# A mixture-of-experts layer on one core: an expert's first table holds 96 places instead of 128

## What is computed

```python
scores = sigmoid(xf @ w_router)                      # 512 tokens x 64 experts
choice = scores + router_bias
# best 4 of 8 groups of experts, then the best TOP_K = 8 experts of those
_, idx = top_k(where(emask, choice, -inf), TOP_K)
wts = sel / sum(sel) * 2.5
routed[tok] = sum over its 8 experts e of  w * ((silu(x @ w_gate_e[e]) * (x @ w_up_e[e])) @ w_down_e[e])
x = layer_norm(ALPHA * x + shared + routed, ln2_g, ln2_b)
```

## Time and profile before

| | us |
|---|---|
| median of 3 runs | 1356.36 (1355.73 to 1359.55) |
| the profiled execution, its own time | 1356.58 |
| its span in the profile | 1355.0 |
| TensorE busy in the span | 1281.0 (95%) |
| VectorE busy | 890.0 (66%) |
| ScalarE busy | 712.3 (53%) |
| GpSimd (POOL) busy | 388.0 (29%) |
| granted TensorE clock, mean | 0.978 of full |

### The profile page before, as it was taken

One profiled execution on the slowest core, in us unless ns is written; L12 is line 12 of the kernel. 1 busy time (PEld: TensorE's weight loads), 2 busy tenths in 40 slices (PEclk: granted clock), 3 DMA queues, 4 the chain that ended last, 5 costly groups with the idle time before them and its releaser, 6 DMA issues.

```text
span 1355.0 us, 15040 instructions
## 1 busy us (share of the span) xinstructions
PE 1281.0 (95%) x5608; PEld 933.7 (69%) x5608; DVE 890.0 (66%) x1167; ACT 712.3 (53%) x870; POOL 388.0 (29%) x262
## 2 busy tenths in 40 slices
PE   7999999999899999987999999999999999999965
PEld 4888766666566775553677787777777777777732
DVE  4011255465756564652688888888888888888858
ACT  4333433333233220011588888888887888887710
POOL 3433322122323351144132332223232222323201
PEclk9999999999999999988999999999999999999978
DMA  4922111111111525040799999999999999999776
GB/s 157 321 82 78 59 59 59 40 58 41 59 40 59 201 78 210 17 156 20 258 378 366 378 366 375 372 373 366 373 373 361 369 367 373 374 366 365 272 317 257
DMA packets 68120, 311.30 MB, mean 230 GB/s; under 512 B 17788, under 2 KB 17916, under 8 KB 41552
## 3 DMA queue, kind: packets, MB, share of 16 engines
q1 hardware_dynamic: 48560, 276.64, 54.8%
q0 software_dynamic: 19488, 33.70, 6.6%
HBM read 305.74 MB, written 42.01 MB: 257 GB/s over the span
## 4 chain that ended last, share of the span: by engine, by line
PE 61%; DMA 25%; DVE 5%; ACT 5%; issue 3%; another core or an unknown queue 0%; POOL 0%; SPq 0%; POOLq 0%; DVEq 0%; ACTq 0%
DMA raw<-in_w_gu 23%; PE PS L655 22%; PE PS L897 8%; PE PS L760 4%; PE PS L847 4%; ACT w_hi_e L1126 4%; PE PS L698 4%; PE PS L850 3%; PE PS L844 3%; PE PS L778 3%; PE PS L731 3%; PE PS L709 2%; PE PS L829 1%; DMA parts<-y_d 1%; PE PS L878 1%
## 5 line engine op out<-in xcount | busy, mean ns | idle before, releaser
L1442 DVE TENSOR_TENSOR w_lo_e<-raw,w_hi_e 128x2048 fp32r<-128x2048 f32 x192 | 433.6, 2282 | 4.9 <-ACT w_hi_e L1126 4.8
L1126 ACT ACTIVATE w_hi_e<-raw 128x2048 fp32r<-128x2048 f32 x192 | 368.4, 1920 | 112.3 <-DMA raw<-in_w_gu 72.0
L1670 POOL DMA_INDIRECT y_d<-y_slots,tab x64 | 113.9, 1779 | 425.7 <-PE PS L916 324.4
L1622 POOL TENSOR_TENSOR w_lo<-ring,w_hi 128x1024 fp32r<-128x1024 f32 x54 | 128.4, 2379 | 292.2 <-ACT w_hi L1028 292.2
L847 PE MATMUL PS<-w_hi_e,xs_lo 128*128 128x512 f32 x512 | 144.7, 404 | 0.0
L844 PE MATMUL PS<-w_hi_e,xs_hi 128*128 128x512 f32 x512 | 143.8, 402 | 0.0
L850 PE MATMUL PS<-w_lo_e,xs_hi 128*128 128x512 f32 x512 | 138.7, 392 | 0.0
L1286 DVE CUSTOM_DVE_ANT_0 region<-PS,region 128x128 f32<-128x128 f32 (+1 forms) x64 | 30.6, 478 | 148.7 <-PE PS L698 146.7
L1071 ACT ACTIVATE region<-region,nmax 128x128 f32<-128x128 f32 (+3 forms) x80 | 43.7, 546 | 149.7 <-DVE nmax L1286 149.5
L655 PE MATMUL PS<-x_hi,w_hi 128*128 128x512 f32 x424 | 115.5, 415 | 0.0
L847 PEld LDWEIGHTS PS<-w_hi_e,xs_lo 128*128 128x128 f32 x512 | 91.7, 188 | 33.5 <-DVE xs_lo L1468 16.2
(11 more groups left out here) (177 smaller groups left out, 1853.1 us busy)
## 6 DMA issues: line engine op xcount, KB each, us to landing
raw<-in_w_gu SPq DMA_DIRECT2D x128, 1024.0 KB, 11.2
raw<-in_w_down_e SPq DMA_DIRECT2D x64, 1024.0 KB, 10.8
ring<-in_w_merge SPq DMA_DIRECT2D x32, 640.0 KB, 3.9
ring<-in_w_proj SPq DMA_DIRECT2D x22, 512.0 KB, 3.7
parts<-y_d SPq DMA_DIRECT2D x8, 1024.0 KB, 15.8
parts<-y_d SPq DMA_DIRECT2D x4, 1536.0 KB, 12.7
region<-in_w_out SPq DMA_DIRECT2D x1, 4096.0 KB, 15.1
bias_d<-bias_rows SPq DMA_DIRECT2D x3, 1280.0 KB, 12.1
```

The costliest lines, as they stand in the source:

```text
L1126: nc.scalar.activation(w_hi_e[b][:, lo:hi], raw[b][:, lo:hi], ACT.Copy).then_inc(made, 1)
L1442: nc.vector.tensor_tensor(w_lo_e[b][:, lo:hi], raw[b][:, lo:hi], w_hi_e[b][:, lo:hi].bitcast(F32), ALU.subtract).then_inc(made, 1)
L1622: nc.gpsimd.tensor_tensor(wl, w, wh.bitcast(F32), ALU.subtract).then_inc(w_lo_made, 1)
L1670: pool.indirect_dma_start(y_d, bass.IndirectOffsetOnAxis(ap=rows, axis=0), y_slots[:, b, :], None, bounds_check=last_row, oob_is_err=False ...
```

## The change

The table of an expert holds `CAP` = 96 places. The tables of 96 places that can be needed for 512 tokens are `N_TAB` = 6 in place of 4; `tab_d` is filled with 576 times 64 pairs in place of 512 times 64. All that has one row of an expert per partition (gather, scatter, `x_slots`, `silu`, `h_rows`, `y_slots`, the outputs of gate_up and down) has 96 partitions; all that has the rows as columns (turned rows and their two parts, turned `h` and its two parts, so the stationary operands of gate_up and down) is 96 columns wide. Number and order of instructions stay in the loop over the experts, as do the weights, their split, and the shared expert. The general loop is entered from a list of 97, in place of 129.

```diff
+CAP = 96
+N_TAB = -(-SEQ // CAP)
+TAB_ROWS = -(-N_TAB * CAP // (P // 2)) * (P // 2)
...
+        def rows_of(s):
+            return P if s < QT else CAP
...
-        tab_d = nc.dram_tensor("tab_d", (SEQ * N_EXP, 2), I32).ap()
+        tab_d = nc.dram_tensor("tab_d", (TAB_ROWS * N_EXP, 2), I32).ap()
...
-                to = PS[:, G_BANK + s % 2, :]
+                to = PS[0:CAP, G_BANK + s % 2, :]
                 for c in cs:
-                    nc.tensor.matmul(to, xs_hi[:, b, c, :], wh[:, c, :], start=(c == 0), stop=False)
+                    nc.tensor.matmul(to, xs_hi[:, b, c, 0:CAP], wh[:, c, :], start=(c == 0), stop=False)
...
-                    mm = nc.tensor.transpose(PS[:, H_BANK, half * P:(half + 1) * P], h_of(s % 2)[:, half, :], ident[:, :])
+                    mm = nc.tensor.transpose(PS[:, H_BANK, half * P:half * P + r], h_of(s % 2)[0:r, half, :],
+                                             ident[0:r, 0:r])
...
-                            mm = nc.tensor.matmul(PS[:, Y_BANK + n, :], hx[:, s % 2, half, :],
+                            mm = nc.tensor.matmul(PS[0:CAP, Y_BANK + n, :], hx[:, s % 2, half, 0:CAP],
                                                   w[:, half, n * 512:(n + 1) * 512],
...
-                xs = x_slots[:, e % 2, :].rearrange("p (q c) -> p c q", c=KT)
+                xs = x_slots[0:CAP, e % 2, :].rearrange("p (q c) -> p c q", c=KT)
                 for c in range(KT):
-                    mm = nc.tensor.transpose(PS[:, X_BANK + c // 4, (c % 4) * P:(c % 4 + 1) * P], xs[:, c, :],
-                                             ident[:, :])
+                    mm = nc.tensor.transpose(PS[:, X_BANK + c // 4, (c % 4) * P:(c % 4) * P + CAP], xs[:, c, :],
+                                             ident[0:CAP, 0:CAP])
...
-                nc.scalar.activation(xs_hi[:, e % 2, :, :],
-                                     PS[:, X_BANK:X_BANK + 2, :].rearrange("p a (c n) -> p (a c) n", n=P), ACT.Copy)\
+                nc.scalar.activation(xs_hi[:, e % 2, :, 0:CAP],
+                                     PS[:, X_BANK:X_BANK + 2, :].rearrange("p a (c n) -> p (a c) n", n=P)[:, :, 0:CAP],
+                                     ACT.Copy)\
...
-            with pe.If(n > P):
+            with pe.If(n > CAP):
...
-            tab_rows = tab_d.rearrange("(c p e) b -> c p e b", p=P, e=N_EXP)
+            tab_rows = tab_d[0:N_TAB * CAP * N_EXP, :].rearrange("(c p e) b -> c p e b", p=CAP, e=N_EXP)
             pool.wait_ge(tab_written, 16 * QT * TOP_K)
-            pool.dma_start(tab[:, :, :], tab_rows[0]).then_inc(tab_in, 16)
+            pool.dma_start(tab[0:CAP, :, :], tab_rows[0]).then_inc(tab_in, 16)
...
-                pool.indirect_dma_start(x_slots[:, b, :], None, x1_d, bass.IndirectOffsetOnAxis(ap=rows, axis=0),
+                pool.indirect_dma_start(x_slots[0:CAP, b, :], None, x1_d, bass.IndirectOffsetOnAxis(ap=rows, axis=0),
                                         bounds_check=last_tok, oob_is_err=False).then_inc(done, 16)
...
-                pool.indirect_dma_start(y_d, bass.IndirectOffsetOnAxis(ap=rows, axis=0), y_slots[:, b, :], None,
+                pool.indirect_dma_start(y_d, bass.IndirectOffsetOnAxis(ap=rows, axis=0), y_slots[0:CAP, b, :], None,
                                         bounds_check=last_row, oob_is_err=False).then_inc(done, 16)
...
-                    scatter(tab[:, e, 1:2], e % 2, rows_out[e % 2])
+                    scatter(tab[0:CAP, e, 1:2], e % 2, rows_out[e % 2])
...
-                    gather(tab[:, j, 0:1], j % 2, slots_in[j % 2])
+                    gather(tab[0:CAP, j, 0:1], j % 2, slots_in[j % 2])
```

More of the change, by code:

```diff
@@ L579, in _ @@
             n = sp.value_load(most_i[0:1, 0:1], min_val=0, max_val=SEQ)
-            with sp.If(n > P):
+            with sp.If(n > CAP):
                 sp.wait_ge(y_done, STEPS_MOE)
-                with sp.Fori(1, SEQ // P) as c:
+                with sp.Fori(1, N_TAB) as c:
                     with sp.Fori(0, N_EXP) as e:
@@ L590, in _ @@
                             .then_inc(ov["w"], 16)
-                sp.wait_ge(ov["out"], 16 * (SEQ // P - 1) * N_EXP)
+                sp.wait_ge(ov["out"], 16 * (N_TAB - 1) * N_EXP)
             for b in range(2):
@@ L965, in _ @@
             n = pe.value_load(most_i[0:1, 0:1], min_val=0, max_val=SEQ)
-            with pe.If(n > P):
+            with pe.If(n > CAP):
                 pe.wait_ge(y_out, N_EXP)
                 pe.sem_inc(ov["y"], 1)
-                with pe.Fori(1, SEQ // P) as c:
+                with pe.Fori(1, N_TAB) as c:
                     with pe.Fori(0, N_EXP) as e:
@@ L980, in _ @@
                         for k in range(KT):
-                            mm = nc.tensor.matmul(PS[:, G_BANK, :], xT[:, k, 0:P], gate_up_of(raw[0])[:, k, :],
+                            mm = nc.tensor.matmul(PS[0:CAP, G_BANK, :], xT[:, k, 0:CAP], gate_up_of(raw[0])[:, k, :],
                                                   start=(k == 0), stop=(k == KT - 1))
@@ L985, in _ @@
                         for half in range(FT):
[L986 to L987 removed]
+                            mm = nc.tensor.transpose(PS[:, H_BANK, half * P:half * P + CAP], h_of(0)[0:CAP, half, :],
+                                                     ident[0:CAP, 0:CAP])
                         mm.then_inc(ov["hturn"], 1)
@@ L1189, in _ @@
             n = act.value_load(most_i[0:1, 0:1], min_val=0, max_val=SEQ)
-            with act.If(n > P):
-                with act.Fori(1, SEQ // P) as c:
+            with act.If(n > CAP):
+                with act.Fori(1, N_TAB) as c:
                     with act.Fori(0, N_EXP) as e:
@@ L1462, in low_hT @@
                 dve.wait_ge(hT_made, s + 1)
-                nc.vector.tensor_tensor(hT_lo[:, s % 2, :, :], PS[:, H_BANK, 0:F].rearrange("p (f n) -> p f n", f=FT),
-                                        hT_hi[:, s % 2, :, :].bitcast(F32), ALU.subtract).then_inc(hT_lo_made, 1)
+                nc.vector.tensor_tensor(hT_lo[:, s % 2, :, 0:CAP],
+                                        PS[:, H_BANK, 0:F].rearrange("p (f n) -> p f n", f=FT)[:, :, 0:CAP],
+                                        hT_hi[:, s % 2, :, 0:CAP].bitcast(F32), ALU.subtract).then_inc(hT_lo_made, 1)
             def low_x(e):
                 dve.wait_ge(xs_hi_made, e + 1)
-                nc.vector.tensor_tensor(xs_lo[:, e % 2, :, :],
-                                        PS[:, X_BANK:X_BANK + 2, :].rearrange("p a (c n) -> p (a c) n", n=P),
-                                        xs_hi[:, e % 2, :, :].bitcast(F32), ALU.subtract).then_inc(xs_lo_made, 1)
+                nc.vector.tensor_tensor(xs_lo[:, e % 2, :, 0:CAP],
+                                        PS[:, X_BANK:X_BANK + 2, :].rearrange("p a (c n) -> p (a c) n", n=P)[:, :, 0:CAP],
+                                        xs_hi[:, e % 2, :, 0:CAP].bitcast(F32), ALU.subtract).then_inc(xs_lo_made, 1)
             def base(t):
@@ L1518, in _ @@
             n = dve.value_load(most_i[0:1, 0:1], min_val=0, max_val=SEQ)
-            with dve.If(n > P):
-                with dve.Fori(1, SEQ // P) as c:
+            with dve.If(n > CAP):
+                with dve.Fori(1, N_TAB) as c:
                     dve.wait_ge(ov["tab"], c * 16)
@@ L1676, in _ @@
             for j in range(2):
-                gather(tab[:, j, 0:1], j, slots_in[j])
+                gather(tab[0:CAP, j, 0:1], j, slots_in[j])
             for s in range(3, STEPS_MOE + 2):
@@ L1689, in _ @@
             n = pool.value_load(most_i[0:1, 0:1], min_val=0, max_val=SEQ)
-            with pool.If(n > P):
+            with pool.If(n > CAP):
                 pool.sem_inc(ov["free"], 1)
-                with pool.Fori(1, SEQ // P) as c:
-                    pool.dma_start(tab[:, :, :], tab_rows[bass.ds(c, 1)].rearrange("c p e b -> (c p) e b"))\
+                with pool.Fori(1, N_TAB) as c:
+                    pool.dma_start(tab[0:CAP, :, :], tab_rows[bass.ds(c, 1)].rearrange("c p e b -> (c p) e b"))\
                         .then_inc(ov["tab"], 16)
@@ L1697, in _ @@
                         pool.wait_ge(ov["rows"], j + 1)
-                        gather(rows_u[:, 0:1], 0, ov["in"])
+                        gather(rows_u[0:CAP, 0:1], 0, ov["in"])
                         pool.wait_ge(ov["yout"], j + 1)
-                        scatter(rows_u[:, 1:2], 0, ov["out"])
+                        scatter(rows_u[0:CAP, 1:2], 0, ov["out"])
                         pool.wait_ge(ov["out"], j * 16 + 16)
```

54 lines of the change are left out of this document (30 added, 24 removed).

## The result

| | us | ratio to before, 95% |
|---|---|---|
| before, median of 4 | 1356.53 (1355.73 to 1359.55) | |
| changed, median of 4 | 1386.59 (1381.06 to 1391.05) | 1.0215 (1.0171 to 1.026) |
| changed, profiled execution | 1384.11, span 1382.5 | |

The account below looks back on a forecast made before the run. The busiest DMA engine, with 8 real rows of each 128, was taken to set the 9.89 us period. 1356.58 - 28.5 (loop) - 0.3 (end) = 1327.8 us profiled, so 1327.5 us predicted, range 1317 to 1357.

Parts of the forecast that it names:

- What bound the kernel before: Expert loop: the DMA engine with 8 real rows of each 128 sets the 9.89 us period; TensorE waits 0.53 us.
- Rows per engine: Gathers and scatters: 96 rows put 6 on each engine; the busiest moves 245,760 bytes, 9.27 us at 26.5 GB/s.
- rival B: Slower: 96 rows go to 8 engines, 12 each, 1431 us; includes blocks of 6 hindering each other; chance 0.06.
- What is late next: Expert loop: TensorE at 9.35 us becomes the bound; period 9.44 us with irregular ones, saving 28.5 us.
- Transposes: TensorE, 10 per expert at 0.112 us: no gain taken, up to 0.28 us per expert if streamed columns count.
- Elementwise: ScalarE and VectorE copies: xs_hi falls by 0.22 us, xs_lo by 0.26, hT copies by 0.05 and 0.07; nothing counted.
- Matmuls: TensorE, 36 per expert: still stream 512 columns, 0.91 us for four; no gain.
- POOL and table: Gathers and scatters may give 0 to 0.7 us of POOL; table fill is 288 KB for 256; nothing counted.
- The end: Last scatter, 3.31 us on the chain: 0.3 us saved by two rows fewer on an engine; result reads untouched.
- A: Rival: rows don't split 6 by 6, the busiest engine keeps 8 real rows, time stays 1356 us; chance 0.20.
- D: Rival: faster than forecast, transposes 0.28 us shorter and rows spread well, 1320 to 1308 us; chance 0.08.
- C: Rival: total bytes bind, not the busiest engine, so time stays 1356 us; chance inside A's 0.20.

Follow-up runs that it names:

- e4: Kernel before, 128 wide, with only the table read back in four reads that spread places over engines and partitions: 1311.42 us, ratio 0.9745.
- e2: Kernel before with the scatters alone cut to 96 partitions: 1332.23 us, ratio 0.9894.
- e1: Kernel before with the gathers alone cut to 96 partitions: 1387.22 us, ratio 1.0299.
- e12: Kernel before with SP's load of the down weights issued as two transfers of 64 partitions: 1688.41 us, ratio 1.2592.
- e8: Kernel before with the gathers alone cut to 112 partitions: 1397.43 us, ratio 1.0291.
- e7: e3b with the places spread over its 96 partitions, against the kernel before: 1322.68 us, ratio 0.9756.
- e3b: Changed kernel, compute 96 wide, but gathers and scatters of 128 partitions, against the kernel before: 1356.84 us, ratio 0.9997.
- e6b: Kernel before with each gather issued as two of 64 partitions, scatters of 128: 1413.51 us, ratio 1.0424.

## Why the prediction was wrong

**What bound the kernel before** was read rightly. That the uneven load, 8 real rows of each transfer on the busiest DMA engine, set the 9.89 us was argued from the earlier trace rows and is borne out by e4: spread the rows, change nothing else, and the period is TensorE's 9.34 us.

**Rows per engine** is the step that failed: "The busiest engine then moves ... 245,760 bytes, 9.27 us at 26.5 GB/s". The count may stand (for the scatter, e2 gains about what it gives), but the rate was taken over from transfers of 128 partitions as if it belonged to the engine. With 96 in the gather the mean packet of both queues grows, weight rows from 346 to 362 ns, rows from 172 to 187, and 9.89 us become 10.32, not 9.27. I had bounded the unknown placement by 9.89 from above; the case that blocks of 6 hinder each other was named in rival B, priced as over 7% of the rate, and dismissed inside its 0.06. e1 shows that a gather of 96 alone is enough for a loss.

The size doesn't close. By the prediction's count an engine would have moved its 245,760 bytes in 10.32 us, 23.8 GB/s, 10% under the 26.5. The mean packets explain about half of it: 16 ns on each of 24 weight rows and 15 on each of 12 rows are 0.56 us, and 1.05 lie between 9.27 and 10.32. Either the slow packets gather on some engines, or the gather still leaves 8 real rows on one: with 8 in the gather and 6 in the scatter it would be 253,952 bytes in 10.32 us, 24.6 GB/s, 7% under, which leaves less to explain. No view gives the packets by engine, so this stays open.

The Trainium skill bears on this step. DMA: Bandwidth & Descriptors (The descriptor swizzle) has each engine of a 128-partition transfer write one port of the SBUF. SBUF — State Buffer (Door 1: The DMA port swizzle) says that DMA bandwidth depends on how many of the 16 ports the partitions reach, and that 32 further partitions stay on the same port. I weighed only whether the first page's formula, cut at 96, leaves 8 rows on an engine, and not what it would cost if two engines came to write one port. By the second page a load of 64 partitions reaches half the ports: e12 agrees in the sign, at 1.26. The 3.0 and 2.9% of e1 and e8, with gathers of 96 and 112, are measured here alone.

**What is late next**: TensorE at 9.35 was right for e4 and e7 (9.34 and 9.38), and never came into play in the changed kernel.

**Transposes**: nothing was taken, and 0.89 us for eight of 96 columns confirm it. **Elementwise**: sizes right (0.81, 0.95, 0.31, 0.36 us), effect none, as e3b shows. **Matmuls**: nothing, but for 0.04 us more per 12 in e7. **POOL and table**: a gather's time fell from 1104 to 969 ns, a scatter's stayed at about 1.8 us, and neither was on the path. **The end**: the last scatter's step in the chain is 3.54 us where 3.31 became 3.0 in the sum; 0.2 us lost, not 0.3 won. The 6.2 us in the block behind it were in no term of the sum. **The general loop** wasn't entered.

**The rivals.** A (no change) and D fell, and so did C (total bytes bound), since e4 moves the same bytes 2.5% faster. B had the sign, and the landings grew past the 12 us that it named, but with another mechanism at its head: the time of 1431 us was for 12 rows on an engine, which e2 speaks against for the scatter, since fewer than 8 per engine is the reading that its gain supports.

What stays open: which partitions exactly an engine serves when there aren't 128, which no view shows; whether it is packets to the same group of partitions that hold each other up, and how; why the rate came out 10% under the one assumed, when the mean packets explain half of it; and the 6.4 us at the end.

## What to carry to other kernels

Where DMAs that write the SBUF run beside each other, try them over all 128 partitions, even when a quarter of them carries nothing: in this kernel the out-of-bounds rows of e3b cost nothing that shows, while narrower gathers and loads cost 3 to 26% (e1, e8, e6b, e12). When the DMA share is near 1 but the bytes are a tenth short, ask which engine has the most real bytes, and deal the real rows out over the engines: four small reads of a table in place of one made this kernel 2.5% faster. And a rate read from one shape of transfer belongs to that shape until a run shows that it holds for another.

## What was unexpected of the hardware

- A gather of 96, 112 or 2 x 64 partitions slows down packets of another queue that have nothing to do with it: 28 to 38% of the weight rows took over 350 ns beside them, 7 to 9% beside gathers of 128. The median weight row hardly changes (309 ns before, 314 in the changed kernel).
- A scatter of 96, which reads the SBUF, does no such harm (6.6% of the weight rows).
- Splitting one of three weight loads by partitions costs 26%, by columns 0.6%.
- The share of busy DMA is no measure of throughput: it is 0.93 at 243 GB/s in e12, 0.98 at 370 before, and 1.00 at 393 in e4.
